# Three 256-column matmuls in place of a 512- and a 256-column one for each turned weight tile

## What is computed

```python
def conv_ffn(h, w_up, conv_w, conv_b, w_down):     # w_up 2048 x 11264, w_down 5632 x 2048
    up = h @ w_up
    padded = jnp.pad(up, ((0, 0), (CONV_WIDTH - 1, 0), (0, 0)))
    conv = conv_b
    for j in range(CONV_WIDTH):
        conv = conv + padded[:, j:j + s] * conv_w[j]
    gate, val = conv[..., :D_FF], conv[..., D_FF:]
    return (jax.nn.silu(gate) * val) @ w_down

# each layer:
h = rms_norm(x, norm_mix_g[i])
x = x + mix(h)                                      # w_in, ..., w_out
x = x + conv_ffn(rms_norm(x, norm_ffn_g[i]), w_up[i], conv_w[i], conv_b[i], w_down[i])
# at the end: rms_norm(x, final_norm_g)
```

## Time and profile of the kernel before

| | |
|---|---|
| median of 3 runs | 2144.76 us (2144.58 to 2144.89) |
| profiled execution, first to last instruction | 2143.7 us |
| TensorE matmul busy | 2118.6 us (99%), 11076 matmuls |
| TensorE weight load busy | 1804.1 us (84%) |
| VectorE busy | 1453.7 us (68%) |
| ScalarE busy | 1043.5 us (49%) |
| mean granted TensorE clock | 0.998 of full speed |
| moved from and to HBM | 394.29 MB read, 2.11 MB written, 185 GB/s |

### The profile page before, as it was taken

How to read it: one execution, slowest core, us unless ns; L and a number is a source line. 1 busy time by engine, 2 the same in 40 slices (tenths; PEclk the granted TensorE clock), 3 DMA queues, 4 the chain that set the end, 5 groups by cost and what they waited for, 6 DMA issues and landing times.

```text
span 2143.7 us, 29615 instructions
## 1 busy us (share of the span) xinstructions
PE 2118.6 (99%) x11076; PEld 1804.1 (84%) x11076; DVE 1453.7 (68%) x1587; ACT 1043.5 (49%) x1078; POOL 30.2 (1%) x59
## 2 busy tenths in 40 slices
PE   7999999999999999999999999999999999999997
PEld 6888888888888888887888888888888888888886
DVE  5786486776767767676556555577776677766776
ACT  6554464445444454455444444464444444444453
POOL 0000000000000000000011000000000000000000
PEclk9999999999999999999999999999999999999999
DMA  8655465555555555654565555555555555555552
GB/s 271 194 172 199 163 198 195 190 182 189 183 195 189 183 189 183 196 180 156 186 192 172 184 183 184 178 179 193 195 177 195 178 194 194 178 195 178 195 189 86
DMA packets 317235, 397.18 MB, mean 185 GB/s; under 512 B 8660, under 2 KB 240380, under 8 KB 317052
## 3 DMA queue, kind: packets, MB, share of 16 engines
q1 hardware_dynamic: 313724, 392.06, 55.9%
q0 software_dynamic: 1056, 3.16, 0.7%
q10 hardware_dynamic: 2400, 1.20, 0.2%
HBM read 394.29 MB, written 2.11 MB: 185 GB/s over the span
## 4 chain that ended last, share of the span: by engine, by line
PE 97%; ACT 1%; DVE 1%; issue 0%; DMA 0%; ACTq 0%; DVEq 0%
PE ps_turned L1249 39%; PE ps_turned L1251 20%; PE ps_straight L1266 12%; PE ps_straight L1268 12%; PE ps_straight L1267 12%; ACT w_high L439 1%; PE ps_turned L1288 1%; PE ps_straight L1457 0%; PE ps_straight L1474 0%; DMA x<-in_x 0%; ACT work L459 0%; DVE w_low L796 0%; PE ps_straight L1466 0%; PE ps_straight L1359 0%; PE ps_straight L1485 0%
## 5 line engine op out<-in xcount | busy, mean ns | idle before, releaser
L1249 PE MATMUL ps_turned<-h_split,w_high 128*128 128x512 f32 x3584 | 1270.0, 399 | 0.0
L796 DVE TENSOR_TENSOR w_low<-w_raw,w_high 128x2048 fp32r<-128x2048 f32 x369 | 845.8, 2293 | 314.6 <-ACT w_high L439 270.6
L1251 PE MATMUL ps_turned<-h_split,w_low 128*128 128x256 f32 x3584 | 1006.1, 281 | 0.0
L439 ACT ACTIVATE w_high<-w_raw 128x2048 fp32r<-128x2048 f32 x369 | 707.4, 1919 | 543.8 <-PE ps_straight L1268 313.5
L1249 PEld LDWEIGHTS ps_turned<-h_split,w_high 128*128 128x128 f32 x3584 | 673.4, 188 | 166.6 <-issue 0.2
L1251 PEld LDWEIGHTS ps_turned<-h_split,w_low 128*128 128x128 f32 x3584 | 676.9, 189 | 1.1
L1266 PE MATMUL ps_straight<-w_high,y_split 128*128 128x512 f32 x960 | 375.5, 391 | 0.0
L1268 PE MATMUL ps_straight<-w_high,y_split 128*128 128x512 f32 x960 | 374.0, 390 | 0.0
L1267 PE MATMUL ps_straight<-w_low,y_split 128*128 128x512 f32 x960 | 373.7, 389 | 0.0
L448 ACT ACTIVATE work<-ps_turned 128x512 f32<-128x512 f32 x112 | 67.1, 599 | 323.3 <-PE ps_turned L1251 277.9
L1268 PEld LDWEIGHTS ps_straight<-w_high,y_split 128*128 128x128 f32 x960 | 180.2, 188 | 38.2
(11 more groups left out here) (184 smaller groups left out, 658.2 us busy)
## 6 DMA issues: line engine op xcount, KB each, us to landing
w_raw<-in_w_up SPq DMA_DIRECT2D x176, 1024.0 KB, 5.1
w_raw<-in_w_down SPq DMA_DIRECT2D x88, 1024.0 KB, 5.1
w_raw<-in_w_in_odd SPq DMA_DIRECT2D x48, 1024.0 KB, 5.4
w_raw<-in_w_in_even SPq DMA_DIRECT2D x24, 1024.0 KB, 5.4
w_raw<-in_w_out_even SPq DMA_DIRECT2D x16, 1024.0 KB, 5.0
w_raw<-in_w_out_odd SPq DMA_DIRECT2D x16, 1024.0 KB, 5.0
x<-in_x SPq DMA_DIRECT2D x4, 512.0 KB, 9.3
work<-c_rows POOLq DMA_DIRECT2D x8, 256.0 KB, 4.5
```

The lines of the kernel that those rows point to most:

```text
L439: a.activation(wh[:, s, :], raw[:, s, :], ACT.Copy).then_inc(s_high, 1)
L796: ve.tensor_tensor(wl[:, s, :], raw[:, s, :], wh[:, s, :].bitcast(F32), ALU.subtract).then_inc(s_low, 1)
L1249: pe.matmul(bank, hi[:, kk, P * m:P * m + P], acts[:, K, :], start=(K == 0), stop=False, skip_group_check=True)
L1251: ins = pe.matmul(bank[:, TOK:], lo[:, kk, P * m:P * m + P], acts[:, K, 0:TOK], start=False, stop=(K == KC - 1), skip_group_check=True)
```

## The change

The 512-column matmul of a turned tile is split in two of 256 columns, and all three products of a tile accumulate into the same 256 columns, the left half of the bank. The loops are exchanged: the tile K is outside, inside it come the three products, and inside these m = 0 and 1, so that neighbouring matmuls go to different banks. Each matmul has its own weight load, as before. The panel is then complete in the left halves, so ScalarE's copy and VectorE's addition are left out for the 112 panels, and a new `take` multiplies straight from PSUM. `take` waits for `s_used` itself; `s_up` and `s_qk` are gone, and their readers wait for `s_added`. The pooling products keep their form. Cut to what matters:

```diff
 # ScalarE: in the mixer of layer 0, the feed-forward blocks and the heads, all of this form
-                    if k in (2, 3, 5, 7):
-                        j = {2: 0, 3: 1, 5: 2, 7: 3}[k]
-                        copy_low_half(Q + j, j % 2, B + k)
 # VectorE
-            def per_token(ap, factor):
-
-                return ve.tensor_tensor(ap, ap, factor.unsqueeze(1).to_broadcast([P, 2, TOK]), ALU.mult)
+            def take(to, q, slot, piece, factor, r=0):
+
+                ve.wait_ge(s_used, at(piece + 1, 12, r))
+                return ve.tensor_tensor(to, psT[:, 2 * slot:2 * slot + 2, 0:TOK],
+                                        factor.unsqueeze(1).to_broadcast([P, 2, TOK]), ALU.mult)
...
-            def take_up(l, j, g, r=0):
+            def take_up(l, j, g, piece, r=0):
 
                 q = Q_FFN[l] + 4 * g + j
-                add_halves(up[:, :, 2:], q, j % 2, r)
-                fenced(per_token(up[:, :, 2:], rstdT[:, :]), s_up, at(44 * l + 4 * g + j + 1, 4, r))
+                fenced(take(up[:, :, 2:], q, j % 2, piece, rstdT[:, :], r), s_added, at(q + 1, 4, r))
 # TensorE, turned_half
-                for m in range(2):
-                    bank = psT[:, 2 * slot + m, :]
-                    for kk in range(8):
-                        K = 8 * k + kk
-                        pe.matmul(bank, hi[:, kk, P * m:P * m + P], acts[:, K, :], start=(K == 0), stop=False,
-                                  skip_group_check=True)
-                        ins = pe.matmul(bank[:, TOK:], lo[:, kk, P * m:P * m + P], acts[:, K, 0:TOK], start=False,
-                                        stop=(K == KC - 1), skip_group_check=True)
+                for kk in range(8):
+                    K = 8 * k + kk
+                    for part, (weights, al) in enumerate(((hi, 0), (hi, TOK), (lo, 0))):
+                        for m in range(2):
+                            ins = pe.matmul(psT[:, 2 * slot + m, 0:TOK], weights[:, kk, P * m:P * m + P],
+                                            acts[:, K, al:al + TOK], start=(K == 0 and part == 0),
+                                            stop=(K == KC - 1 and part == 2))
                 ins.then_inc(s_used, 1)
```

More of the change, by code:

```diff
@@ L237, in build @@
         s_vr = sem("v_ready")
-        s_qk = sem("qk_ready")
         s_sc = sem("scores_done")
@@ L439, in high, with copy_low_half @@
                 a.activation(wh[:, s, :], raw[:, s, :], ACT.Copy).then_inc(s_high, 1)
[L441 to L448, removed]
+            def copy_low_half(j, piece=None):
+                if piece is not None:
+                    a.wait_ge(s_used, piece + 1)
+                if j:
+                    a.wait_ge(s_added, Q_WPOOL + j)
+                bank = 2 * (j % 2)
+                fenced(a.activation(spare, psA[:, bank:bank + 2, TOK:], ACT.Copy), s_spare, j + 1)
             def squares(s, n):
@@ L525, in gelu_u @@
             def gelu_u(j):
-                a.wait_ge(s_u, j + 1)
+                if j:
+                    a.wait_ge(s_added, Q_U[j] + 1)
+                else:
+                    a.wait_ge(s_u, 1)
                 fenced(a.activation(ub, ub, ACT.Gelu), s_gelu, j + 1)
@@ L562, in _ @@
                             a.wait_ge(s_wp, j + 1)
-                        copy_low_half(Q_WPOOL + j, 0, n if j == 3 else None, bank=2 * (j % 2))
+                        copy_low_half(j, n if j == 3 else None)
                     for j in (0, 1) if n < N_WPOOL else (2, 3):
@@ L579, in scale_last_tap @@
                 q = 44 * l + 4 * g + j
-                a.wait_ge(s_up, at(q + 1, 4, r))
+                a.wait_ge(s_added, at(Q_FFN[l] + 4 * g + j + 1, 4, r))
                 if j % 2 == 0 and q >= 2:
@@ L665, in ffn @@
                         act_high(l, 1, g, c - 5, to=1)
-                    if k < 8 and k % 2:
-                        copy_low_half(Q + 4 * g + k // 2, (k // 2) % 2, c + k)
                     if k == 10 and l == 1:
@@ L796, in low, with add_halves @@
                 ve.tensor_tensor(wl[:, s, :], raw[:, s, :], wh[:, s, :].bitcast(F32), ALU.subtract).then_inc(s_low, 1)
[L798 to L802, removed]
-            def per_token(ap, factor):
-                return ve.tensor_tensor(ap, ap, factor.unsqueeze(1).to_broadcast([P, 2, TOK]), ALU.mult)
+            def add_halves(to, j):
+                ve.wait_ge(s_spare, j + 1)
+                bank = 2 * (j % 2)
+                fenced(ve.tensor_tensor(to, psA[:, bank:bank + 2, 0:TOK], spare, ALU.add), s_added, Q_WPOOL + j + 1)
+            def take(to, q, slot, piece, factor, r=0):
+                ve.wait_ge(s_used, at(piece + 1, 12, r))
+                return ve.tensor_tensor(to, psT[:, 2 * slot:2 * slot + 2, 0:TOK],
+                                        factor.unsqueeze(1).to_broadcast([P, 2, TOK]), ALU.mult)
             def split_low(y, src, high_done, count, signal):
@@ L889, in pool_windows @@
                 W = 2 << j
-                add_halves(pp[:, :, 16:], Q_POOL + j, j % 2)
-                link(per_token(pp[:, :, 16:], rstdT[:, :]))
+                fenced(take(pp[:, :, 16:], Q_POOL + j, j % 2, N_POOL + 2 * j + 1, rstdT[:, :]), s_added, Q_POOL + j + 1)
                 src, bufs = pp, [pb, pa] if j % 2 else [pa, pb]
@@ L917, in u_ready @@
             def u_ready(j):
-                add_halves(ub, Q_U[j], j % 2)
-                fenced(per_token(ub, rstdT[:, :]), s_u, j + 1)
+                fenced(take(ub, Q_U[j], j % 2, N_U[j][1], rstdT[:, :]), s_added, Q_U[j] + 1)
             def gate(j):
@@ L975, in _ @@
                 if n == N_U[0][1]:
-                    add_halves(gt, Q_U[0], 0)
+                    fenced(take(gt, Q_U[0], 0, n, rstdT[:, :]), s_added, Q_U[0] + 1)
                 if n in (N_WPOOL - 1, N_WPOOL):
                     for j in (0, 1) if n < N_WPOOL else (2, 3):
-                        add_halves(wp_sum[j % 2], Q_WPOOL + j, 0, bank=2 * (j % 2))
+                        add_halves(wp_sum[j % 2], j)
                     for j in (0, 1) if n < N_WPOOL else (2, 3):
@@ L1048, in ffn @@
                     if k in (2, 3, 5, 7):
-                        take_up(l, {2: 0, 3: 1, 5: 2, 7: 3}[k], 0)
+                        take_up(l, {2: 0, 3: 1, 5: 2, 7: 3}[k], 0, B + k)
                 with ve.Fori(0, NG - 2) as r:
@@ L1069, in ffn @@
                         if k in (1, 3, 9, 11):
-                            take_up(l, {1: 0, 3: 1, 9: 2, 11: 3}[k], 1, r)
+                            take_up(l, {1: 0, 3: 1, 9: 2, 11: 3}[k], 1, c + k, r)
                         if 4 <= k < 8:
@@ L1098, in ffn @@
                     if k < 8 and k % 2:
-                        take_up(l, k // 2, g)
+                        take_up(l, k // 2, g, c + k)
                     if l == 1 and k >= 14:
@@ L1115, in _, with take_qk @@
             ffn(0)
-            def take_qk(j, first, r=0):
+            def take_qk(j, first, piece, r=0):
                 q = Q_MIX1 + 4 * first + j
-                buf = qk[j // 2][j % 2]
-                add_halves(buf, q, j % 2, r)
-                fenced(per_token(buf, rstdT[:, :] if j % 2 else q_rstdT), s_qk, at(4 * first + j + 1, 4, r))
+                fenced(take(qk[j // 2][j % 2], q, j % 2, piece, rstdT[:, :] if j % 2 else q_rstdT, r),
+                       s_added, at(q + 1, 4, r))
             def head_logits(hh, bank, r=0):
@@ L1193, in heads_of_group @@
                     if k in (5, 7, 9, 11):
-                        take_qk((k - 5) // 2, first, r)
+                        take_qk((k - 5) // 2, first, c + k, r)
             heads_of_group(0)
@@ L1452, in scores @@
                 pair = (hh // 2) % 2
-                pe.wait_ge(s_qk, at(4 * group + 2 * pair + 2, 4, r))
+                pe.wait_ge(s_added, at(Q_MIX1 + 4 * group + 2 * pair + 2, 4, r))
                 qT, kT = qk[pair]
@@ L1574, in _ @@
                 if n == 0:
-                    pe.wait_ge(s_qk, 16)
+                    pe.wait_ge(s_added, Q_MIX1 + 16)
                     attend(13, psT[:, 1, :], 3)
```

16 lines of the change are left out of this document (1 added, 15 removed).

## The result

The changed kernel takes 2169.13 us (median of 4 runs, 2168.79 to 2169.50) against 2144.67 us for the kernel before on the same chip: ratio 1.0113, 95% interval 1.0101 to 1.0125. It is slower by 24.5 us. The forecast had the direction and a range that holds the time, but its size, 93 us, is almost four times too large.

What follows compares the result with a forecast made beforehand. TensorE's unbroken row of matmuls was taken as the bound. The third matmul added 93.2 us to the 2143.7 us span, all other parts 0, giving 2236.9; with 1.1 us to the median, 2238.0 us, range 2158 to 2275.

Steps and rivals of the forecast that it cites:

- The bound: Whole kernel: TensorE's gapless row of matmuls sets the time, busy 2118.6 of 2143.7 us, with waits of 12.9 us.
- The removed copies and additions: 112 ScalarE copies and 112 VectorE additions, 67.1 and 77.4 us busy, hidden behind TensorE's matmuls: 0 us on the path.
- The moved order: Turned tiles: neighbouring matmuls alternate between two banks; a change of bank neither saves nor costs, 0 us.
- the moved wait: `take` on VectorE's queue waits for TensorE instead of ScalarE's copy; TensorE waits for neither bank nor panel: 0 us.
- The price of the third matmul: 3584 turned tiles: three matmuls at 126.4 ns, 379.2 in place of 353.2, 26.0 ns more a tile, +93.2 us.
- every matmul pays 13 ns whatever its size: TensorE matmuls: 13 ns beyond the columns at 2.4 GHz, with some 6.8 more where a full load has 256-column cover.
- Rival 1: Turned tiles: the added matmul pays only a small fixed share, 20.1 to 44.4 us, 2165 to 2189; chance 0.25.
- Line 1382: 32 float32 128-column matmuls with full loads, starts 111.5 ns apart: cheapest bound, -67.0 us; set aside for half-pace streaming.
- The Trainium skill's rule: Issue gap N / 2.4 + 2.5 ns: pair 325 ns against 353.2 traced, so not holding; its share alone 9 us, 2154.

Runs made afterwards that it cites:

- the split alone: The kernel before, with only the 512-column matmul split into two of 256, ScalarE's copy and VectorE's addition left in: 2168.93 us, ratio 1.0112.
- the run in one bank: The changed kernel with the loop over m outside again, so 24 matmuls in a row accumulate into one bank's same 256 columns: 2168.92 us, ratio 1.0113.
- the run with small loads: The changed kernel with 16 of 128 weight columns in all matmuls of a tile except the first that fills the bank: 2102.58 us.

## Why the prediction was right or wrong

**The bound: right.** Matmuls in an unbroken row set the time before and after, and the waits of TensorE are the same. The page's busy time, the stretches and the runs all put the difference at 23 to 25 us.

**The removed copies and additions: right.** Priced at 0; the split alone, with all of them in place, takes as long as the changed kernel.

**The moved order and the moved wait: right.** Alternating banks was priced at 0 from one change of bank, and the run in one bank agrees. VectorE waits for TensorE in its place, and TensorE has no wait for `take` (line 791):
```profile
429.75 0.69 DVE L791 TENSOR_TENSOR work<-ps_turned,rstd_rows 128x512 f32<-128x512 f32 x1 [1.52 <-PE ps_turned L1230]
```

**The price of the third matmul: wrong in size, 93.2 us for 24.5.** The step that failed is the difference 353.2 - 226.8 = 126.4 ns, read as the price of a 256-column matmul with a full load, and multiplied by three. The runs take the pair apart in another way:

| part of a tile, ns | pair of before | three of 256 |
|---|---|---|
| 768 columns, no load in the way | 340.3 (226.8 + 113.5) | 340.5 (3 x 113.5) |
| full loads behind 256 columns | 1: 6.9 | 3: 19.4 |
| the rest of the pair's excess | 6.0 | 0 |
| sum | 353.2 | 359.9 |

The 6.9 is 353.2 - 346.3; the 6.0 is the remainder, 346.3 - 340.3; the 19.4 is 359.9 - 340.5. The change added two full loads behind 256 columns (12.5 ns) and took away the 6.0 ns that only unlike pairs pay. These 6.0 ns aren't the price of alternating as such: the run with a small load behind the 256-column matmul has them from its ninth pair on and not in the first eight. A pair of unlike matmuls doesn't give the price of either: my difference charged the 6.0 ns to the 256-column matmul, and so multiplied by three a cost that the change removes. The term that was to be 126.4 ns measured 120.0, and 3584 x 3 x 6.4 ns = 69 us is the miss. The sentence that every matmul pays 13 ns whatever its size is false as well: 113.5 and 226.8 ns are in the ratio of their columns. I had no row of equal 256-column matmuls, and put the two unknown parts in the term that the change multiplies. The split of the pair is book-keeping: its parts don't simply add, since a small load behind the 512-column matmul saves 3.2 ns of the 12.9 (353.2 - 340.3) as well.

The prediction had the load in its argument: 109 ns of streaming for 128 weight columns against 107 of cover. That a full load costs time behind 256 columns is shown (113.5 ns with small loads, 120.0 with full ones), and its price, 6.8 ns there, was close too (6.5 measured). The reason given is not shown: the 256 columns take 113.5 ns, so that by this reckoning the load would have 4 ns to spare.

**Rival 1 came nearest**: 119.6 ns a matmul, 2165 us. But its 119.6 is the pair with small loads less 226.8, that is 113.5 and the 6 ns that unlike pairs pay; that it lies beside the 120.0 of equal matmuls with full loads is chance. Its reason, a price that doesn't depend on the load, is refuted by the run with small loads. Its unlike neighbours do cost something, but that is the other 6 ns, not the 6.8 that it named.

**Line 1382: rightly put aside**, for streaming at half the pace; line 1474 bears this out with 215 ns for 256 float32 columns.

**The Trainium skill's rule** ("TensorE: Matmul & The Clock Gate", "Back-to-back issue gap"), N / 2.4 + 2.5 ns for the gap of a matmul without its load, would give 109.2 ns for 256 columns, an estimate. The least pace that any run showed for these fp32r matmuls is 113.5 ns, with small loads, so the measurement decides against it here.

## What to carry to other kernels

When TensorE is the bound, count the weight loads and what covers each: here a 128-column load behind 512 moving columns was free among equal matmuls (226.8 ns) and cost up to 3.2 ns in a mixed pair, behind 256 it cost 6.5 ns, and behind 128 it set the pace at 110 ns. Splitting a matmul to save work on engines with slack bought nothing. Where full loads stand behind short matmuls, put matmuls of equal length next to one another, which gave 1.0% here without any other edit; and a price taken as the difference of a mixed row is only good for the same mix.

## What the runs showed of the hardware that I had not expected

- fp32r columns cost 0.443 ns at a granted clock of 1.00 (226.8 ns for 512, 113.5 for 256), 6% more than the 0.417 ns of one column a cycle at 2.4 GHz, in proportion to the columns.
- Going from 512-column matmuls to 256 and back costs some 20 ns net with full loads: eight of 512 take 1.84 us where 1.81 is the pace, eight of 256 take 0.95 where 0.96 is. A mixed pair pays some 6 to 7 ns beside the load's price, but in the run with a small load behind 256 columns not from the start: eight pairs at 340 ns, then 347, with the change at the first full load behind 256 columns. What happens there stays open.
- A 256-column matmul with a full load takes 120.0 ns, although matmuls of 128 columns with full loads follow one another at 110 ns. So the price isn't simply the longer of load and columns. Why it is 120 and not 113.5, and why the small load behind the 512-column matmul took half of the pair's excess away (350.0 ns), stays open. No run here varied the load's width between 16 and 128 or the columns between 256 and 512.
